# Keys transposed in 32x32 blocks on VectorE and regrouped through memory, with the state products and outputs one unit later

## The reference, cut to what matters

```python
def step(S, blk):
    qb, kb, vb, gb = blk
    b = jnp.cumsum(gb, axis=2)
    ref = b[:, :, C // 2:C // 2 + 1]
    b_last = b[:, :, C - 1:C]
    scores = jnp.einsum('bhtd,bhsd->bhts', qb * jnp.exp(b - ref), kb * jnp.exp(ref - b))
    scores = jnp.where(causal, scores, 0.0)
    o = (jnp.einsum('bhts,bhsv->bhtv', scores, vb)
         + jnp.einsum('bhtd,bhdv->bhtv', qb * jnp.exp(b), S))
    S = (jnp.exp(b_last[:, :, 0])[..., None] * S
         + jnp.einsum('bhsd,bhsv->bhdv', kb * jnp.exp(b_last - b), vb))
    return S, o
```

## Time and profile before

| | |
|---|---|
| Median of 3 runs | 1391.1 us |
| Profiled execution, its own time | 1389.28 us |
| Its span from first to last instruction | 1387.6 us |
| PE busy | 1372.1 us, 99% |
| DVE busy | 921.9 us, 66% |
| ACT busy | 687.5 us, 50% |
| POOL busy | 241.6 us, 17% |
| Mean granted clock of TensorE | 0.997 |

### The profile page before, as it was taken

How to read it: one execution, slowest core, us unless ns; L and a number is a source line. 1 busy time by engine, 2 the same in 40 slices (tenths; PEclk the granted TensorE clock), 3 DMA queues, 4 the chain that set the end, 5 groups by cost and what they waited for, 6 DMA issues and landing times.

```text
span 1387.6 us, 21227 instructions
## 1 busy us (share of the span) xinstructions
PE 1372.1 (99%) x8368; PEld 1358.0 (98%) x8368; DVE 921.9 (66%) x1538; ACT 687.5 (50%) x1016; POOL 241.6 (17%) x240
## 2 busy tenths in 40 slices
PE   9999999999999999999999999999999999999997
PEld 8999999999999999999999999999999999999997
DVE  7989655668874446688744567887445688974443
ACT  6565544355664343555633445565334455653332
POOL 2113121110131211111212110112220201130001
PEclk9999999999999999999999999999999999999998
DMA  6433533245335333453263334443533465534328
GB/s 201 126 109 113 204 123 118 95 128 185 107 107 205 122 121 107 123 171 121 96 219 108 121 108 137 154 127 107 205 120 97 133 165 172 159 112 170 111 103 96
DMA packets 97443, 187.52 MB, mean 135 GB/s; under 512 B 49088, under 2 KB 57664, under 8 KB 95680
## 3 DMA queue, kind: packets, MB, share of 16 engines
q1 hardware_dynamic: 97344, 186.16, 42.5%
HBM read 170.72 MB, written 15.42 MB: 134 GB/s over the span
## 4 chain that ended last, share of the span: by engine, by line
PE 93%; DVE 5%; ACT 1%; issue 1%; DVEq 0%; ACTq 0%
PE Z L484 29%; PE Z L486 28%; PE Z L485 28%; PE B L635 1%; DVE wlo L992 1%; PE B L539 1%; PE B L625 1%; DVE xres L1335 1%; PE B L516 1%; DVE h_b L1032 0%; PE B L576 0%; DVE fac L1055 0%; PE B L751 0%; ACT L857 0%; PE B L615 0%
## 5 line engine op out<-in xcount | busy, mean ns | idle before, releaser
L992 DVE TENSOR_TENSOR wlo<-wraw,whi 128x1024 fp32r<-128x1024 f32 x280 | 367.3, 1312 | 324.0 <-ACT whi L763 323.7
L484 PE MATMUL Z<-hhi,whi 128*128 128x416 f32 x1576 | 554.3, 352 | 0.0
L486 PE MATMUL Z<-hhi,wlo 128*128 128x416 f32 x1576 | 549.4, 349 | 0.0
L485 PE MATMUL Z<-hlo,whi 128*128 128x416 f32 x1576 | 549.4, 349 | 0.0
L763 ACT ACTIVATE whi<-wraw 128x1024 fp32r<-128x1024 f32 x280 | 295.3, 1056 | 424.6 <-PE Z L486 404.9
L484 PEld LDWEIGHTS Z<-hhi,whi 128*128 128x128 f32 x1576 | 296.0, 188 | 1.6 <-issue 0.8
L485 PEld LDWEIGHTS Z<-hlo,whi 128*128 128x128 f32 x1576 | 296.1, 188 | 0.4
L486 PEld LDWEIGHTS Z<-hhi,wlo 128*128 128x128 f32 x1576 | 295.9, 188 | 0.2
L486 PE MATMUL Z<-mhi,wlo 128*128 128x416 f32 x320 | 112.3, 351 | 0.0
L485 PE MATMUL Z<-mlo,whi 128*128 128x416 f32 x320 | 111.9, 350 | 0.0
L484 PE MATMUL Z<-mhi,whi 128*128 128x416 f32 x320 | 111.5, 348 | 0.0
(11 more groups left out here) (240 smaller groups left out, 1667.6 us busy)
## 6 DMA issues: line engine op xcount, KB each, us to landing
wraw<-w_all SPq DMA_DIRECT2D x280, 512.0 KB, 3.5
xres<-xT SPq DMA_DIRECT2D x5, 1664.0 KB, 7.3
xin<-xT SPq DMA_DIRECT2D x4, 1664.0 KB, 8.0
yT<-xres SPq DMA_DIRECT2D x4, 1664.0 KB, 8.2
v_blocks<-h_vt SPq DMA_DIRECT2D x80, 52.0 KB, 2.5
vtm<-v_blocks SPq DMA_DIRECT2D x20, 192.0 KB, 3.4
s<-s_in SPq DMA_DIRECT2D x4, 512.0 KB, 5.8
ss_out<-snew SPq DMA_DIRECT2D x4, 512.0 KB, 5.4
```

The lines of the kernel that those rows point to most:

```text
L484: pe.matmul(out, wh, xh, start=first, stop=False)
L485: pe.matmul(out, wh, xl, start=False, stop=False)
L486: return pe.matmul(out, wl, xh, start=False, stop=final)
L992: dve.tensor_tensor(wlo[n % RING][:], raw(t, n)[:], whi[n % RING][:].bitcast(F32), ALU.subtract).then_inc(wlo_made, 1)
```

## The change

The transposes of the keys leave PE and ACT. DVE transposes `kj4` (and `e4`'s last 32 columns) in 32x32 blocks, SP writes them with four DMAs of 52 KB to a second buffer in memory, in its slot 4h+8, and reads them back into `ktm` in its slot 4h+10 with two DMAs. In the last tile the 32 sample columns are still transposed by PE. The products of the states move from unit 4h+8 to 4h+9, the outputs and ACT's squares from 4h+9 to 4h+10, DVE's `split_squares` from slot 4h+10 to 4h+11. `updates(h-1)` moves between the first two products of `queries` and the copies into `fac`. `decayed_keys` moves from slot 4h+5, behind its `wlo`, to the end of slot 4h+4. `output` moves to the end of its slots. The values are read back in SP's slot 4h+10. The banks of the pooling products are exchanged, and in the last tile the sample's pieces move one slot.

```diff
@@ SP
                         if s == 4 * h + 7:
                             values_out(t, h)
-                        if s == 4 * h + 9:
+                        if s == 4 * h + 8:
+                            keys_out(t, last, h)
+                        if s == 4 * h + 10:
                             values_in(t, last, h)
+                            keys_in(t, last, h)
...
+            def keys_out(t, last, h):
+
+                n = t * H + h
+                rows_out = PT if last else T
+                sp.wait_ge(kt_made, n + 1)
+                if n:
+                    sp.wait_ge(ktm_landed, k_value(t, last, h - 1) if h else 32 * n)
+                for a in range(4):
+                    sp.dma_start(k_mem[0:rows_out, a * CHUNK:(a + 1) * CHUNK].rearrange("(c i) j -> i c j", i=CHUNK),
+                                 kt[a * CHUNK:(a + 1) * CHUNK, 0:rows_out].rearrange("p (c j) -> p c j", j=CHUNK)
+                                 ).then_inc(k_kept, 16)
+
+            def keys_in(t, last, h):
+
+                n = t * H + h
+                sp.wait_ge(k_kept, n * 64 + 64)
+                sp.wait_ge(p_done, t * H + h * (3 if last else 1))
+                sp.dma_start(ktm[:, 0:NG, :], k_mem[0:PT].rearrange("(g p) v -> p g v", p=P)).then_inc(ktm_landed, 16)
+                if not last:
+                    sp.dma_start(ktm[0:SAMPLE, 3, :], k_mem[PT:T]).then_inc(ktm_landed, 16)
@@ PE
                     if s == base + 7:
-                        pe.wait_ge(kj_made, nth(t, KJ * H, KJ * h + KJ - 1))
-                        if not h:
-                            pe.wait_ge(ybm_made, t * G)
-                        elif last:
-                            pe.wait_ge(s_made, s_value(t, last, h - 1, NG + 3))
-                        else:
-                            pe.wait_ge(ktm_made, nth(t, H, h - 1))
-                        transposes(B7, kj4[:].rearrange("p g j n -> p (g j n)"), tk_done, e4)
+                        pe.wait_ge(kj_made, nth(t, KJ * H, KJ * h + 1))
+                        if last:
...
+                            pe.transpose(B7[0:SAMPLE, 3 * P:4 * P], e4[:, PT:T], ident[:]).then_inc(tk_done, 1)
...
-                    if s == base + 8:
-                        pe.wait_ge(ktm_made, nth(t, H, h))
+                    if s == base + 9:
+                        pe.wait_ge(ktm_landed, k_value(t, last, h))
                         pe.wait_ge(vtm_landed, 32 * nth(t, H, h))
...
-                    if s == base + 9:
+                    if s == base + 10:
                         outputs(t, last, h)
@@ ACT
             def decays(t, last, h):
                 act.wait_ge(z_sem("f", h), z_done(t, "f", h))
+                act.wait_ge(k_kept, 64 * (t * H + h))
...
-                        if s == 4 * h + 7:
-                            act.wait_ge(tk_done, nth(t, H, h))
-                            rest = B7[0:SAMPLE, 3 * P:4 * P]
-                            act.activation(ktm[:, 0:3, :], B7[:, 0:3 * P].rearrange("p (g v) -> p g v", v=P), ACT.Copy)
...
-                        if s == 4 * h + 9:
+                        if s == 4 * h + 10:
                             act.wait_ge(o_done, nth(t, H, h))
@@ DVE, queries
                 dve.tensor_tensor(e1[:], qf[h % 2][:], e1[:], ALU.mult).then_inc(q_made, 1)
 
+                if h:
+                    updates(t, last, h - 1)
                 d = chunk_decay(h)
@@ DVE, decayed_keys
                 decayed(kj4[:, 1, ::-1], k2[:, 1], end[:, 1])
+                dve.wait_ge(k_kept, 64 * (t * H + h))
+                dve.wait_ge(kj_made, nth(t, KJ * H, KJ * h + KJ - 1))
+                ins = dve.transpose(kt[:, 0:PT], kj4[:].rearrange("p g j n -> p (g j n)"))
+                if not last:
+                    ins = dve.transpose(kt[:, PT:T], e4[:, PT:T])
+                ins.then_inc(kt_made, 1)
@@ DVE, tile
-                    if 5 <= s <= 8 and not first(t):
-                        output(t - 1, range(2 * s - 10, 2 * s - 8))
-                    if s % 4 == 2 and 10 <= s <= 22:
-                        h = (s - 10) // 4
+                    if s % 4 == 3 and 11 <= s <= 23:
+                        h = (s - 11) // 4
                         dve.wait_ge(osq_made, nth(t, H, h))
...
-                            if h and not last:
-                                updates(t, last, h - 1)
                             sums(t, last, h)
-                            if h and last:
-                                updates(t, last, h - 1)
-                            queries(t, h)
-                        if s == 4 * h + 5:
-                            decayed_keys(t, h)
+                            queries(t, last, h)
...
+                    if s % 4 == 0 and 4 <= s <= 16:
+                        decayed_keys(t, last, s // 4 - 1)
...
+                    if s == 4 * H + 4:
+                        updates(t, last, H - 1)
+                    if 5 <= s <= 8 and not first(t):
+                        output(t - 1, range(2 * s - 10, 2 * s - 8))
```

More of the change, by code:

```diff
@@ L87 @@
             B4_USES.append(("scores", _h))
-        if _s == 4 * _h + 9:
+        if _s == 4 * _h + 10:
             B5_USES.append(("o", _h))
@@ L174, in step_kernel @@
         og = [buf["og0"], buf["og1"]]
+        kt = put("kt", [T], F32, hg[names.index("logf")])
         vt, logf, bc, dd, dl = buf["vt"], buf["logf"], buf["b"], buf["d"], buf["dl"]
@@ L266, in step_kernel @@
         B4, B5, B6, B7 = [ctx.enter_context(nc.psum_tensor(f"B{i}", [P, 512], F32)) for i in range(4, 8)]
+        k_mem = nc.dram_tensor("k_blocks", (T, P), F32, kind="Internal").ap()
         v_mem = nc.dram_tensor("v_blocks", (T, P), F32, kind="Internal").ap()
@@ L364, in p_value, with k_value @@
             return t * H + h * (3 if last else 1) + i + 1
+        def k_value(t, last, h):
+            return 32 * t * H + (16 if last else 32) * (h + 1)
         def win_value(t, last, g, level, sample=False):
@@ L418, in tile @@
                         sp.dma_start(exts[:, :, :, 0:BUF], buf_in).then_inc(buf_landed, 16)
-                    if last and s in (13, 17, 21, 25):
-                        h = (s - 13) // 4
+                    if last and s in (14, 18, 22, 26):
+                        h = (s - 14) // 4
                         sp.wait_ge(s_made, s_value(t, last, h, NG + NB - 1))
@@ L545, in small @@
                             sample_products(h, B7, vms[0])
-                    if s == base + 9:
+                    if s == base + 10:
                         outputs(t, last, h)
-                    if s == base + 9 and last:
+                    if s == base + 10 and last:
                         pe.wait_ge(s_made, s_value(t, last, h, NG - 1))
@@ L557, in small @@
                     pe.wait_ge(pml_made, nth(t, G, g))
-                    if g == 1:
-                        pe.wait_ge(ktm_made, nth(t, H, H - 1))
-                    if g < 2:
+                    if g == 0 and last:
+                        pe.wait_ge(s_made, s_value(t, last, H - 1, NG + 3))
+                    elif g == 0:
+                        pe.wait_ge(ybm_made, t * G)
+                    elif g == 1:
                         pe.wait_ge(s_made, s_value(t, last, H - 1, NG + NB - 1 if last else 3))
@@ L572, in small @@
                     y_squares(t - 1, False)
-            def transposes(bank, src, done, rest):
-                for g in range(NG):
-                    pe.transpose(bank[:, g * P:(g + 1) * P], src[:, g * P:(g + 1) * P], ident[:])
-                pe.transpose(bank[0:SAMPLE, 3 * P:4 * P], rest[:, PT:T], ident[:]).then_inc(done, 1)
             def sample_products(h, bank, v):
@@ L833, in tile @@
                             sigmoid(t, "g", h, ga[h % 3], sg_made)
-                        if s == 4 * h + 7:
-                            act.wait_ge(tk_done, nth(t, H, h))
-                            rest = B7[0:SAMPLE, 3 * P:4 * P]
-                            act.activation(ktm[:, 0:3, :], B7[:, 0:3 * P].rearrange("p (g v) -> p g v", v=P), ACT.Copy)
-                            if last:
-                                high_rows(ks, rest, 1).then_inc(ktm_made, 1)
-                            else:
-                                act.activation(ktm[0:SAMPLE, 3, :], rest, ACT.Copy).then_inc(ktm_made, 1)
                         if s == 4 * h + 7 and last:
+                            act.wait_ge(tk_done, h + 1)
+                            high_rows(ks, B7[0:SAMPLE, 3 * P:4 * P], 1).then_inc(kh_made, 1)
                             act.wait_ge(so_done, h + 1)
@@ L845, in tile @@
                                            ACT.Copy).then_inc(so_made, 1)
+                        if s == 4 * h + 8 and last:
                             act.wait_ge(vtm_landed, 32 * nth(t, H, h))
                             high_rows(vs[h // 2], vtm[0:SAMPLE, 3, :], 2).then_inc(split_v, 1)
-                        if s == 4 * h + 9:
+                        if s == 4 * h + 10:
                             act.wait_ge(o_done, nth(t, H, h))
```

(17 more changed lines are left out.)

29 lines of the change are left out of this document (20 added, 9 removed).

## The result

The changed kernel takes 1439.9 us, median of runs from 1437.8 to 1441.4; the kernel before, on the same chip, takes 1390.7. The ratio is 1.0354, with a 95% interval of 1.0336 to 1.0372. It is slower, as forecast, but by 49 us where 23 were forecast, and it lies 13 us above the range.

What follows compares the result with a forecast made beforehand. PE, busy 99% of the span, was taken to bound the kernel. 1389.3 - 12.5 (PE's part) + 23.6 (unit 12 stalls) + 4 (smaller collisions) + 8 (clock) = 1412.4; with 1.8 for the median, 1414 us, range 1386 to 1427.

Steps and rivals of the forecast that it cites:

- PE's part: On PE, dropping the key transposes and the wait before the last tile's outputs gains 12.5 us in all.
- The term of 10.1 us: PE's saving from the dropped transposes: 16 heads at 0.53 us and four last-tile heads at 0.4.
- The 2.4 us of `carry`: PE's waits before the last tile's outputs, in three places, would go because updates have a whole unit more: 2.4 us.
- DVE's part: On DVE, per head: block transposes cost 0.8 us more, the copies into `fac` 1.1 us less.
- The walk to unit 12: Second tile followed from slot 4: late store, key writes and weights stall PE 5.9 us at unit 12, 23.6 in four tiles.
- if issuing the key writes is held up as well: Upper bound of the stall at unit 12: some 3 us more, 9 us.
- Smaller collisions: Slots 12 to 20, without a store: a stall of nearly nothing, taken as 0.8 us per tile, 4 in all, bounds 0 and 10.
- The clock: PE's clock falls in each of the four stalls at unit 12, costing 2 us per stall, 8 in all.
- The whole gain: Rival: unit 14's weights or the squares are ready in time and 12.5 us come off, 1379 us; chance 0.16.
- it decides as soon as the last outputs are made before about 332: Condition in slot 8 under which the whole gain would arrive: last outputs made before about 332 on the profile's clock.
- The rival that the store leaves the weights alone: The 1664 KB store does not delay weight reads; stall 1.9 us in four tiles, no clock fall, 1390 us; chance 0.14.
- The worst case: Key writes in 128-byte rows hold up the queue; stalls of 9 us, waits at heads 2 and 3, 1426 to 1432; chance 0.12.

Runs made afterwards that it cites:

- no transposes: The kernel before without its key transposes on PE (but the last tile's sample) and their copies on ACT, state products multiplying zeros: 1382.7 us.
- the last version: Changed kernel with squares, scores' copy, pooling and means' low halves and sample updates earlier on DVE, outputs at old place, store later in tiles 2 to 4: 1380.7 us.
- squares first: The changed kernel with the split of the squares and the copy of the scores ahead of the slot's low part of the weights on DVE: 1403.6 us.
- outputs early: The changed kernel with the multiplications of the last outputs back at their old place in slots 5 to 8: 1421.0 us.
- the weights first: The changed kernel with the weights loaded ahead of the key writes in SP's slots 8, 12, 16 and 20: 1415.9 us.

## Why the prediction was right in direction and wrong in size

**PE's part: right, and mis-sized.** The transposes went and nothing else on PE changed. The term of 10.1 us measured 7 alone as time and 8.5 as PE's busy time (no transposes), 8.2 in the last version (1372.1 - 1363.9). The forecast took the distance from the transposes to the scores, 0.53. But without them the scores follow the last matmul of unit 6 by 0.28 us (314.37 to 314.65 in the last version), where the transposes had followed it by 0.19 (314.80 to 314.99). A head saves 0.44, for 16 heads 7.0. The 2.4 us of `carry` went as forecast; waits for `snew` and `vms` in the same tile replaced them.

**DVE's part: right.** The block transposes take 0.58 and 0.17 us, together 0.75 against 0.8; the first is shorter than both prices that the forecast weighed for it, 0.66 and 0.93; the copies into `fac` took 0.82 in place of 2.10, 1.28 less against a forecast of 1.1.

**The walk to unit 12: right mechanism, its sum right by compensation.** Four stalls were forecast at 5.9 and measured 7.1, 7.3, 6.4 and 3.9, 24.7 against 23.6. In the second tile, with 6.4 us taken off the times of the profile after: the store was forecast at 334.3 and issued at 335.6; weights 14 were forecast in at 344.3 and ACT began on them at 345.1. Two things on the way were missed. The key writes were priced at 1.9 us like those of the values; behind the store their issuing took 4.32, which the bound for "if issuing the key writes is held up as well" allowed for. And the squares' matmul waits for two things. The forecast followed the squares and overlooked that their bank is read by the scores' copy, which stands one step behind them and ends 0.7 us later. That copy stood behind the low half of the same weights before the change too, with 2.6 us to spare; the sentence that nothing there depended on this `wraw` was true of the squares and false of the place. Both omissions make the stall longer; the last tile, which keeps less of it, brings the sum back.

**Smaller collisions: the step that failed.** The forecast failed at two terms that belong together, this one and the clock below it: they were 14.2 and 9.5 us too small, 23.7 of the 26.7 us by which the difference of the spans (49.8 against 23.1) was missed. The smaller collisions were taken as 4 us in all, with an upper bound of 10. The waits outside these four places and outside the start and the end come to some 18 us: 6.5 in the first tile, 7.8 at unit 20, 4.0 for the last tile's sample states. The forecast had looked for them by walking one tile that has a store. The first tile has none and was not walked at all, though there the key writes stand ahead of the weights as well, and `scale` stands on DVE in addition; with squares first its part fell to 1.7 us, so it is mostly the same order on DVE. For the sample states of the last tile the forecast saw only that the outputs had a unit more; what now came late were the states' own updates, and with these ahead of the weights in the last version 4.0 us became 1.5 (`snew` and `vms`). At unit 20 the walk had found a margin of nothing and priced it at nearly nothing. The two parts of the split ran beside POOL's window sums there (DVE, then POOL, changed kernel):

```profile
401.64 1.08 DVE L1359 CAST sqh<-h_osq 128x416 fp32r<-128x416 f32 x1
402.75 1.17 DVE L1361 TENSOR_TENSOR sql_head<-h_osq,sqh 128x416 fp32r<-128x416 f32 x1
```

```profile
400.94 1.53 POOL L1500 TENSOR_TENSOR pa<-ext 128x430 f32<-128x430 f32 x1 [7.83 <-ACT ext L899]
402.56 0.91 POOL L1500 TENSOR_TENSOR pb<-pa 128x428 f32<-128x428 f32 x1
```

They took 2.25 us where they take 0.96 at unit 12, which is half of that wait of 2.6.

**The clock: right mechanism, too small.** Priced at 2 us for each of four stalls, 8; the same matmuls took 17.5 us more in all. For the four stalls the price was nearly right: their stretches at 0.50 cost 2.7, 2.1, 2.1 and 2.7 us, 9.6 in all. What the forecast left out are four more places, unit 12 of the first tile (a wait of 3.5) and unit 20 of tiles 2 to 4 (2.2 to 3.0), at 1.5 to 1.7 us each, 6.6 in all. It had tied the fall of the clock to the long stalls and priced the small waits without it. In the second tile, for one, the stretch from 400 to 420, around a wait of 2.6 us, is at 0.91. By the Trainium skill (TensorE: Matmul & The Clock Gate, Part 1) the clock halves after idling and returns only after sustained work; the trace agrees, with 0.50 kept for 5.4 us after the long wait ended. Which of the short waits pay is settled only in part. In the twelve traces, start and end of the kernel left out, a stretch at 0.50 goes with all 12 waits of 3.5 us and more, with 15 of 22 between 2.0 and 3.1, and with 2 of 47 between 1.0 and 2.0. Some of these stretches begin up to 1.4 us after the wait has ended, with PE at work again.

**The account.** -8.2 of transposes, -2.4 of old waits, +24.7 at the four places, +18.2 of other waits (what is left of the 40.5 of idle time) and +17.5 of slower matmuls (16.2 of them found in stretches at 0.50) give 49.8 us, the difference of the two spans. The forecast had -10.1, -2.4, +23.6, +4 and +8.

**The rivals.** The whole gain does not arrive, but "it decides as soon as the last outputs are made before about 332" fell too: with outputs early the store leaves at 333.9 in a run that lies 6.3 us later at this tile, so they are made by 327.6 of the profile before, and 3.0 us of wait remain. The rival that the store leaves the weights alone fell with the weights first: directly behind the store they took 6.7 us to land, close to the 6.4 that the forecast had taken from a load. The worst case (key writes hold up the queue) is the one nearest to what happened, and was 8 to 14 us too low, for want of the small waits and their clock. The slow issuing is not due to the keys' rows of 128 bytes alone: in the kernel before with the outputs moved, two reads of values behind the store took 1.21 and 1.41 us to issue, where they take 0.38 and 0.48. How much of the 4.32 us is the store's work in the queue and how much the memory's behind it was not separated.

## What to carry to other kernels

When a step is moved on an in-order engine, list everything that stands behind the next wait on that engine, not only the moved step: here two small steps behind one late load cost 36 us; put ahead of it, they made PE wait no more at that place. Ask of each consumer all that it waits for, its PSUM bank's earlier reader too. Count a price of the clock for waits of 2 to 3 us as well, not only for long stalls. When a slower version has the right instructions and only its waits are too long, put its steps in a better order before judging the change: the same instructions ran in 1439.9 and in 1380.7 us.

## What the runs showed of the hardware that was not expected

Four DMA issues of 52 KB each took 4.32 us on SP's queue when a store of 1664 KB had been issued 0.46 us ahead of them, 1.90 when it had been issued 8.3 us ahead, and 1.87 with none near. A load of 512 KB issued 1.1 us behind that store landed after 6.7 us, where 3.5 is the median. Thirty-four matmuls with no use, in each of three stalls, made the kernel 7.8 us faster. Waits of PE between 2.0 and 3.1 us were followed by a fall of its clock in 15 of 22 cases, and the same place in the second tile shows both: a fall at a wait of 2.95 us, none at one of 2.75. And on DVE a conversion of 128x416 took 1.08 us beside POOL's additions and 0.37 without. The Trainium skill (GPSIMD Engine Reference, Specifications) says that GpSimd shares its SBUF interfaces with VectorE and contends with DVE instructions that have two SBUF inputs or run in a 2-port performance mode. The subtraction beside POOL, with two inputs, agrees with it: 1.17 us against 0.59. The conversion has one input and was slowed as well; by the page that would be the 2-port mode, and no trace here shows which mode an instruction ran in.
